# A mixture-of-experts stage: the first gate-up ahead of the routing tables, the first gather ordered by tokens, half of the shared gate-up moved

## The reference: what is computed

```python
scores = sigmoid(h @ w_router)                     # 256 tokens, 64 experts
sel = scores + bias; keep 4 of 8 groups, then the top 6 experts of each token
w = scores of the chosen / their sum * 2.5
for each expert e:                                  # sparse: only its own tokens
    y = (silu(g) * u) @ w_down[e],  g, u = split(h[tokens of e] @ w_gate_up[e])
    routed[tokens of e] += w * y
shared = swiglu(h, shared_gate_up, shared_down)     # every token
x = x + gate * (routed + shared)
```

## Time and profile before

| | |
|---|---|
| time, median of 3 runs | 1317.53 us (1315.44 to 1317.74) |
| time of the profiled execution | 1317.53 us |
| its span | 1315.7 us |
| mean granted TensorE clock | 0.94 |
| PE busy | 1093.1 us (83%) |
| DVE busy | 440.4 us (33%) |
| ACT busy | 256.6 us (20%) |
| moved by DMA | 502.26 MB, mean 382 GB/s |

### The profile page before, as it was taken

One profiled execution on the slowest core, in us unless ns is written; L12 is line 12 of the kernel. 1 busy time (PEld: TensorE's weight loads), 2 busy tenths in 40 slices (PEclk: granted clock), 3 DMA queues, 4 the chain that ended last, 5 costly groups with the idle time before them and its releaser, 6 DMA issues.

```text
span 1315.7 us, 17277 instructions
## 1 busy us (share of the span) xinstructions
PE 1093.1 (83%) x6664; PEld 609.6 (46%) x6664; DVE 440.4 (33%) x1028; ACT 256.6 (20%) x572; POOL 0.4 (0%) x5
## 2 busy tenths in 40 slices
PE   5999999998787878777679989999878877877766
PEld 4887577543333424333237567744433332423332
DVE  1297775222112112112137867622111212211213
ACT  1122523111001111011022472311100101100100
POOL 0000000000000000000000000000000000000000
PEclk9999899999899999889789999999978989988988
DMA  9999987999999999999996847599999999999995
GB/s 349 383 402 409 339 307 305 401 425 422 422 425 424 423 423 424 424 425 422 423 351 261 312 168 272 236 401 425 423 423 424 424 423 423 423 425 423 423 423 206
DMA packets 100170, 502.26 MB, mean 382 GB/s; under 512 B 11865, under 2 KB 37366, under 8 KB 44790
## 3 DMA queue, kind: packets, MB, share of 16 engines
q1 hardware_dynamic: 99622, 500.92, 93.5%
q10 hardware_dynamic: 464, 0.20, 0.1%
HBM read 500.04 MB, written 1.05 MB: 381 GB/s over the span
## 4 chain that ended last, share of the span: by engine, by line
SPq 43%; PE 35%; DMA 11%; DVE 5%; issue 4%; ACT 2%; DVEq 0%; ACTq 0%
SPq L601 40%; PE bank L738 27%; DMA ring<-in_moe_w_gate_up 6%; SPq L691 3%; PE bank L1151 2%; PE bank L741 2%; DMA w_gu_x<-in_moe_w_gate_up 2%; DMA w_gu<-in_moe_w_gate_up 2%; PE bank L840 1%; PE bank L982 1%; DMA ring<-in_ada_w 1%; ACT p_sb L1386 1%; PE bank L1132 1%; PE bank L905 1%; DVE s_sb L1662 0%
## 5 line engine op out<-in xcount | busy, mean ns | idle before, releaser
L738 PE MATMUL bank<-w_gu,ring 128*32 128x512 f32 (+1 forms) x1088 | 338.4, 692 | 86.2 <-DMA w_gu<-in_moe_w_gate_up 58.1
L738 PEld LDWEIGHTS bank<-w_gu,ring 128*32 128x32 f32 (+1 forms) x1088 | 88.9, 133 | 218.2 <-issue 218.2
L738 PE MATMUL bank<-ring 128*32 128x512 f32 (+1 forms) x384 | 164.6, 709 | 23.9 <-DMA w_gu<-in_moe_w_gate_up 23.9
L1814 DVE TENSOR_TENSOR hh<-sg,bank 128x256 f32<-128x256 f32 x44 | 27.3, 621 | 465.0 <-ACT sg L1419 465.0
L738 PE MATMUL bank<-w_gu_x,ring 128*32 128x512 f32 (+1 forms) x320 | 137.8, 646 | 24.3 <-DMA w_gu<-in_moe_w_gate_up 20.0
L738 PE MATMUL bank<-w_gu,hhT 128*32 128x512 f32 (+1 forms) x576 | 147.0, 599 | 0.4 <-DMA w_gu<-in_moe_w_down 0.4
L1419 ACT ACTIVATE sg<-bank 128x256 f32<-128x256 f32 x44 | 16.9, 385 | 538.5 <-PE bank L738 538.5
L738 PE MATMUL bank<-w_dn,ring 128*32 128x512 f32 x240 | 96.2, 772 | 25.6 <-DMA w_gu<-in_moe_w_gate_up 10.3
L1831 DVE SCALAR_TENSOR_TENSOR y_lo<-bank,w_slot,y_hi 128x512 fp32r<-128x512 f32 x88 | 66.1, 751 | 132.5 <-ACT y_hi L1309 132.5
L738 PE MATMUL bank<-sel,h_hi 128*128 128x256 f32 x352 | 87.7, 289 | 0.0
L738 PE MATMUL bank<-sel,h_lo 128*128 128x256 f32 x352 | 84.2, 279 | 0.0
(11 more groups left out here) (291 smaller groups left out, 1552.7 us busy)
## 6 DMA issues: line engine op xcount, KB each, us to landing
w_gu<-in_moe_w_gate_up SPq DMA_DIRECT2D x126, 1024.0 KB, 25.9
w_gu<-in_moe_w_down SPq DMA_DIRECT2D x68, 1024.0 KB, 26.3
ring<-in_moe_w_gate_up SPq DMA_DIRECT2D x44, 1024.0 KB, 26.7
w_gu_x<-in_moe_w_gate_up SPq DMA_DIRECT2D x38, 1024.0 KB, 25.3
ring<-in_ada_w SPq DMA_DIRECT2D x36, 1024.0 KB, 9.7
w_dn<-in_moe_w_gate_up SPq DMA_DIRECT2D x30, 1024.0 KB, 25.7
ring<-in_moe_w_down SPq DMA_DIRECT2D x16, 1024.0 KB, 26.1
w_dn<-in_moe_w_down SPq DMA_DIRECT2D x14, 1024.0 KB, 26.8
```

The lines of the kernel that those rows point to most:

```text
L738: return nc.tensor.matmul(o, a, b, start=first, stop=last)
L1814: v.tensor_tensor(hh[:, :].rearrange("s (f p) -> s p f", f=FE // P), sg[:, :].rearrange("s (p f) -> s p f", f=FE // P), bank[b][:, FE:2 * ...
```

## The change

On PE three things move in `experts(l)`, in both layers. The first gather runs token half by token half (`gather_first`) rather than feature half by feature half, and starts as soon as half 0 of `h_lo` is there. The product for `order` and both halves of `gate_up(0)` come directly behind it, ahead of the other table products. `shared_gate_up(0, 1, 6)` moves from ahead of the gather to between the halves of `gate_up(1)`. On DVE the second half of `h_lo` comes behind `select(0)`. On SP the load of expert 4's down matrix comes behind the loads of pass 2. On ACT the silu of the shared part comes behind that of pass 0, and a small activation that loads the silu table stands in its old place. Some PSUM banks change with it.

```diff
@@ SP
-                fixed_loads(l, LAST_UNITS)
+                fixed_loads(l, LAST_UNITS[0:1])
                 sp.wait_ge(sem("order"), l + 1)
...
+                    if n == 0:
+                        fixed_loads(l, LAST_UNITS[1:])
@@ PE
-                shared_gate_up(0, 1, 6)
...
+                def gather_first():
+                    pe.wait_ge(sem(f"sel_ready{l}"), 1)
+                    for ti in range(NT):
+                        pe.wait_ge(sem("h_act"), 4 * l + 2 * ti + 2)
+                        pe.wait_ge(sem("h_dve"), 4 * l + 2 * ti + 2)
+                        for half, banks in enumerate(((4, 7), (0, 1))):
+                            for kk in range(4):
+                                o = bank[banks[kk // 2]][:, (kk % 2) * N:(kk % 2 + 1) * N]
+                                for h in (h_hi, h_lo):
+                                    last = nc.tensor.matmul(o, h[:, ti, 4 * half + kk, :], sel[:, ti, :],
+                                                            start=ti == 0 and kk % 2 == 0 and h is h_hi,
+                                                            stop=ti == NT - 1 and h is h_lo, skip_group_check=True)
+                            if ti == NT - 1:
+                                last.then_inc(sem(f"gath_done{l}"), 1)
...
                 def gate_up(p, halves=(0, 1)):
-                    pe.wait_ge(sem(f"xg_ready{l}"), 2 * (p // 2) + 2)
-                    if p == 0:
-                        pe.wait_ge(sem("order"), l + 1)
-                    elif p >= 2:
+                    if p >= 2:
                         pe.wait_ge(sem(f"st_ready{l}"), p)
                     for half in halves:
+                        pe.wait_ge(sem(f"xg_ready{l}"), half + 1 if p == 0 else 2 * (p // 2) + 2)
...
-                pe.wait_ge(sem("h_act"), 4 * l + 4)
-                pe.wait_ge(sem("h_dve"), 4 * l + 4)
-                gather_half(0, 0)
-                gather_half(0, 1, (2, 3))
+                gather_first()
+                pe.wait_ge(sem("flags"), 2 * l + 1)
+                mm(bank[2][0:1, 0:E], const("row")[0:E, :], hot[:, :], True, True).then_inc(sem("order_ps"), 1)
+                gate_up(0)
...
-                gate_up(0)
-                gate_up(1)
+                pe.wait_ge(sem("order"), l + 1)
+                gate_up(1, (0,))
+                shared_gate_up(0, 1, 6)
+                gate_up(1, (1,))
@@ ACT
+                nc.scalar.activation(small[:, 34:35], eps_c, ACT.Silu)
+                gathered(0, 0)
+                gathered(0, 1, (0, 1))
+                silu(0, GU_BANK[0])
                 after(("sgu", l, 0))
...
-                gathered(0, 0)
-                gathered(0, 1, (2, 3))
-                silu(0, GU_BANK[0])
@@ DVE
-                for j in range(4):
-                    dve.wait_ge(sem("h_act"), 4 * l + j + 1)
-                    v.tensor_tensor(interleaved(h_lo, j), in_order(bank[j]), interleaved(h_hi, j).bitcast(F32), ALU.subtract)\
-                        .then_inc(sem("h_dve"), 1)
+                low_parts(0, 2)
...
                 select(0)
-
+                low_parts(2, 4)
```

More of the change, by code:

```diff
@@ L687, in _ @@
                 fixed_loads(l, LATE_UNITS)
-                fixed_loads(l, LAST_UNITS)
+                fixed_loads(l, LAST_UNITS[0:1])
                 sp.wait_ge(sem("order"), l + 1)
-                for items in LOADS:
+                for n, items in enumerate(LOADS):
                     index = {j: sp.value_load(tab_i[0:1, j:j + 1], min_val=0, max_val=E - 1)
@@ L934, in experts, with gather_half @@
                 last.then_inc(sem("counts"), 1)
-                shared_gate_up(0, 1, 6)
-                def gather_half(i, half, banks=(4, 7)):
+                def gather_first():
[12 more added lines that the diff above has]
+                                last.then_inc(sem(f"gath_done{l}"), 1)
+                def gather_half(i, half):
                     pe.wait_ge(sem(f"sel_ready{l}"), i + 1)
                     for kk in range(4):
-                        o = bank[banks[kk // 2]][:, (kk % 2) * N:(kk % 2 + 1) * N]
+                        o = bank[(4, 7)[kk // 2]][:, (kk % 2) * N:(kk % 2 + 1) * N]
                         for ti in range(NT):
@@ L1022, in shared_down @@
                     last.then_inc(sem("shared_done"), 1)
-                pe.wait_ge(sem("h_act"), 4 * l + 4)
-                pe.wait_ge(sem("h_dve"), 4 * l + 4)
-                gather_half(0, 0)
-                gather_half(0, 1, (2, 3))
+                gather_first()
+                pe.wait_ge(sem("flags"), 2 * l + 1)
+                mm(bank[2][0:1, 0:E], const("row")[0:E, :], hot[:, :], True, True).then_inc(sem("order_ps"), 1)
+                gate_up(0)
                 pe.wait_ge(sem("w_of"), l + 1)
-                pe.wait_ge(sem("sh_g"), l + 1)
                 for ti in range(NT):
-                    tr(bank[6][0:E, ti * P:(ti + 1) * P], slot_of[:, ti, :])
+                    tr(bank[3][0:E, ti * P:(ti + 1) * P], slot_of[:, ti, :])
                 for ti in range(NT):
-                    last = tr(bank[6][0:E, N + ti * P:N + (ti + 1) * P], w_of[:, ti, :])
+                    last = tr(bank[3][0:E, N + ti * P:N + (ti + 1) * P], w_of[:, ti, :])
                 last.then_inc(sem("tabT_ps"), 1)
-                pe.wait_ge(sem("flags"), l + 1)
-                mm(bank[5][0:1, 128:128 + E], const("row")[0:E, :], hot[:, :], True, True).then_inc(sem("order_ps"), 1)
+                pe.wait_ge(sem("flags"), 2 * l + 2)
                 mm(bank[1][0:E, 128:131], const("tri")[0:E, 0:E], flag[:, 0:3], True, False)
@@ L1060, in experts @@
                 mm(bank[1][0:1, 192:192 + OVER], const("row")[0:E, :], onehot[:, 4, :], True, True).then_inc(sem("over_ps"), 1)
+                pe.wait_ge(sem("sh_g"), l + 1)
                 middle(0)
@@ L1719, in experts, with low_parts @@
                 v.tensor_tensor(chosen[:, :, :], left[:, :, 0:E], choice[:, :, 0:E], ALU.not_equal).then_inc(sem("chosen"), 1)
-                for j in range(4):
-                    dve.wait_ge(sem("h_act"), 4 * l + j + 1)
-                    v.tensor_tensor(interleaved(h_lo, j), in_order(bank[j]), interleaved(h_hi, j).bitcast(F32), ALU.subtract)\
-                        .then_inc(sem("h_dve"), 1)
+                def low_parts(n0, n1):
+                    for j in range(n0, n1):
+                        dve.wait_ge(sem("h_act"), 4 * l + j + 1)
+                        v.tensor_tensor(interleaved(h_lo, j), in_order(bank[j]), interleaved(h_hi, j).bitcast(F32), ALU.subtract)\
+                            .then_inc(sem("h_dve"), 1)
+                low_parts(0, 2)
                 dve.wait_ge(sem("ranks"), l + 1)
@@ L1771, in experts @@
                 link(V, v.tensor_reduce(rank[:, 0:1], keys[:, 1, :], AX_X, ALU.add))
-                v.tensor_scalar(hot[:, :], const("rank_of", E), rank[:, 0:1], None, ALU.is_equal)
+                v.tensor_scalar(hot[:, :], const("rank_of", E), rank[:, 0:1], None, ALU.is_equal).then_inc(sem("flags"), 1)
                 v.tensor_scalar(rank[:, 1:2], rank[:, 0:1], float(LAST_WIDE) + 0.5, -32.0, ALU.is_lt, ALU.mult)
@@ L1790, in experts @@
                 dve.wait_ge(sem("order_ps"), l + 1)
-                v.tensor_copy(tab_i[:, 0:E], bank[5][0:1, 128:128 + E]).then_inc(sem("order"), 1)
+                v.tensor_copy(tab_i[:, 0:E], bank[2][0:1, 0:E]).then_inc(sem("order"), 1)
                 dve.wait_ge(sem("tabT_ps"), l + 1)
-                v.tensor_copy(flat(rtT[:, :, :]), bank[6][0:E, :]).then_inc(sem("tabT"), 1)
+                v.tensor_copy(flat(rtT[:, :, :]), bank[3][0:E, :]).then_inc(sem("tabT"), 1)
                 dve.wait_ge(sem("places"), l + 1)
```

## The result

| | before | after |
|---|---|---|
| median of 14 runs each | 1317.04 us (1311.6 to 1322.08) | 1322.89 us (1319.26 to 1327.24) |
| ratio, 95% interval | | 1.0048 [1.0032, 1.0064] |
| span of the profiled execution | 1315.7 us | 1323.1 us |
| mean granted clock | 0.940 | 0.936 |

The change makes the kernel slower by about 6.3 us (4.2 to 8.4), where 3.5 us were predicted. The execution that was profiled took 1324.94 us, about 2 us above the median; that of the kernel before took 1317.53 us, 0.5 above.

A forecast was written before the change was run, and what follows sets the result against it. PE's end of down(1) plus fixed DMA bytes sets each mixture's time. Waits of 1.56 and 0.39 less 0.19 make 1.76 us per layer, 3.5 in all: 1317.53 becomes 1321.0 us, range 1316.5 to 1324.5.

The forecast's parts named there:

- What bounds the kernel: Each mixture's time is when PE ends down(1), releasing SP's next load, plus a fixed quantity of bytes by DMA.
- Rival B: Early expert loads count: 4.26 us less idle DMA per layer is kept, 8.5 us go, time 1309.0; chance 7%.
- the 4.26 us: gate_up(0) and SP's first pair of loads come this much earlier per layer; forecast to buy nothing.
- First wait: PE ahead of the first gather: making sel is no longer hidden behind the shared products, 1.56 us of new idle time.
- rival D: PE's new idle time costs its full clock: 1.65 us a layer, 1322.7 in one, 1324.3 in both; chance 13%.
- A: Forecast's main case, slower because down(1) ends 1.76 us later per layer: 1321.0 us, own range 1319.5 to 1322.8; chance 55%.
- The order of the work: PE up to the end of gate_up(1): 1.76 us late per layer, from 1.56 + 0.39 - 0.19; at most 2.6.
- Rival C: PE catches up as waits vanish or the selection is ready sooner: 2 x 1.0 us or less, 1317.5 to 1319.5; chance 25%.
- SP and DMA: First pair issued at 220.46, load behind down(1) at 253.11; DMA hole grows from 1.8 to 3.8 us, 1.7 ahead of it.

The follow-up runs named there:

- e4: Changed kernel with SP's pass-2 loads held back until both halves of gate_up(0) are done: 1323.25 us, ratio 1.0041.
- e8: Kernel before with eight useless products (3.45 us of PE work) added ahead of the shared half, no idle time: 1325.06 us, ratio 1.0071.
- e2: Changed kernel with the shared half moved back behind the count products, ahead of the gather: 1318.46 us, ratio 1.0010.
- e1: Changed kernel with three useless products filling PE's idle time ahead of the gather: 1321.68 us, ratio 1.0037.
- e9: Kernel before with nine useless products in PE's idle time between the layers, ahead of the norm's transposes: 1316.76 us, ratio 0.9993.
- e6: Changed kernel with the first gather by feature halves again, behind the whole of h_lo: 1326.9 us, ratio 1.0081.
- e10: Changed kernel with nine useless products in PE's idle time between the layers, ahead of the norm's transposes: 1320.29 us, ratio 1.0021.

## Why the prediction was right, and where its sizes were off

**What bounds the kernel** held in full. The change made the first pair of loads earlier and the release later, and the time followed the release. Of the 7.4 us by which the spans differ, 0.1 lie ahead of layer 0's count products, 3.57 between them and layer 1's (836.10 before, 839.77 after), and 3.73 behind; the shifts of the releases are 3.62 and 3.55. e4 shows the half of it that speaks against early loads, e8 the half that speaks for PE's time. Rival B is refuted by e4, where B would have the 4.9 us paid, and by e2, where 2.3 us of earlier loads bring nothing. The rule that a DMA be issued early (the Trainium skill, DMA: Bandwidth & Descriptors, Rules for kernel authors) gains nothing for these ten loads, since DMA waits out what they gain. What it gives as its reason is only that the fixed setup cost overlaps with the compute, so the 4.26 us that the prediction read into it are more than it says.

**First wait** (1.56 us): right. The gather starts at 2.86 where 2.93 was forecast, with 1.42 us of idle time in the row, which counts from the modelled end of the last count product.

**The clock** is the step that failed. It was rival D with 13%, priced 1.65 us a layer; the row of 1.74 us of idle time with a fall behind it was set aside since the new gap would be shorter. In the profiled execution it fell in both layers, for 3.3 us each, and cost 1.34 (layer 0) and 1.28 us (45.44 less 44.16). That is less than half of 3.3: in layer 0 15 products of the gather fall into the stretch, each 0.10 us slower, 1.5 us in all, and 0.15 of these come back because PE, being slower, no longer has to wait for the second half of `h_lo` (see below). The forecast's own case, A, is the one without a fall, and its range ended at 1322.8, just under the median of 1322.89. The median is close to D in one layer (1322.7), the profiled execution to D in both (1324.3 forecast, 1324.94 measured). So the direction and the mechanism of the release were right for the reason given, but that the time lies in the range is owed to its having been widened for D. Part of the nearness to 1322.7 is luck: D took the order of the work too low and the clock too high.

**The order of the work** was to cost 1.76 us a layer, at most 2.6, and costs 2.28 (e1). By the prediction's own numbers the upper bound is 1.76 - 0.39 + 1.09 = 2.46, not 2.6, which changes nothing here. Measured from the count products without a fall of the clock, term by term:

| term | forecast | e1 |
|---|---|---|
| gate_up(0) starts | 7.14 | 7.28 |
| gate_up(0) | 6.94 | 7.02 |
| tables | 2.54 | 2.43 |
| half 0 of gate_up(1) | 3.47 | 3.59 |
| shared half | 3.48 | 3.65 |
| half 1 of gate_up(1) | 3.47 | 3.58 |
| end of gate_up(1) | 27.04 | 27.55 |

From the gather's start to gate_up(0) it takes 4.41 us where 4.21 was taken, and the gather began 0.06 earlier: 0.14 us. gate_up(0) does follow ACT's copy of feature half 0 as forecast, but ACT's row in e1

```profile
215.84 2.06 ACT L1327 ACTIVATE ring<-bank 128x512 f32<-128x512 f32 x4 [5.87 <-PE bank L950]
```

begins 3.27 us behind the gather (215.84 less 212.57), where 3.10 was forecast. Nearly all of that is seen in PE's rows of e1 above: at the change to the second token half it is 0.20 us from 214.43 to 214.63 and 0.19 to 214.82, instead of 0.12 each, 0.15 us in all. DVE finished this half's `h_lo` only at 214.49 (212.44 and 2.05 us). The forecast had it ready 0.14 us ahead of PE. The largest part, 0.40 us, is the shared half between the halves of gate_up(1): each of the three groups costs 0.11 to 0.17 us more than it did in its old place, the halves of gate_up in a row and the shared half ahead of the gather. That the change of shape is the reason is argued, not tested. I had costed a moved group at its length in its old place.

**Rival C** (PE catches up) is refuted: no wait of the stretch vanished, and only that for rtT shrank, from 0.35 to 0.23 us. Waits of PE from 203 to 286 us after the change (us in total, times, longest), which answer to the earlier trace rows:

```profile
PE bank L947 <- DVE sel L1768: 1.4, 1, 1.4
PE bank L996 <- DVE y_lo L1851: 0.4, 1, 0.4
PE bank L740 <- DVE chosen L1735: 0.2, 1, 0.2
PE bank L740 <- DVE rtT L1813: 0.2, 1, 0.2
```

**SP and DMA**: the forecast issues (220.46, 233.3, 236.8, 244.4, 253.11) came at 222.03, 234.97, 238.71, 246.35 and 255.07, late by 1.6 to 2.0 us, which is the clock (1.3), the terms of the table, and 0.1 by which the whole mixture starts later. The hole has the predicted 3.8 us; the one ahead of it is 0.9 us instead of 1.7.

**What stays open.** The executions of one kernel differ by up to 12 us (before, beside e9: 1312.11 to 1324.19), and the difference of two profiled executions between layer 0's and layer 1's count products goes beyond the shift of the mixture by up to 5.3 us (e8: 635.42 against 626.64 before, with a shift of 3.45). In the records this goes roughly with the time at half clock between 650 and 760 us (4.4 us in e9, 9.3 before, 16.1 in e8, 20.5 in e6), but e8 has the largest difference and not the longest time. e9 was made to take it away and shows no measurable gain, so the cause of the spread is argued, not shown.

## What to carry to other kernels

Where DMA has a hole and then never stops, find the last release of a buffer ahead of the saturated stretch: only the time of that one is paid, and loads issued earlier widen the hole. Work that looks free to move may be the cover of a wait: price the wait that it uncovers, then the clock behind it. A short idle gap of PE can cost its length plus what the engine loses at half clock. With products in the gap, even useless ones, the profile of e1 has no such loss, though the medians don't resolve it.

## What the hardware showed that I had not expected

- 1.42 us of idle PE time was followed by a granted clock of 0.50 for 3.3 us (212.4 to 215.7) in five of the six mixtures of after, e4 and e10, and by 1.00 in the sixth, layer 1 of e10. The 16 mixtures without the gap had 1.00 there.
- Groups of products of different shape in turn took longer here than in a row: a half of gate_up 3.47 us (from its start to that of the next group, mean of four) next to its like and 3.59 beside the shared products (e1).
